# Four sums of weight blocks: from GpSimd additions to accumulating DMAs

## The reference, cut to what matters

```
x = x + mix                     # out_proj "rg_out" (layer 0), "sb_out" (layer 1)
h = rmsnorm(x, norm_ffn_g[layer])
g = h @ w_gate ; u = h @ w_up   # 1024 -> 2816
x = x + (silu(g) * u) @ w_down  # 2816 -> 1024
```

## Time and profile before

| what | value |
|---|---|
| median of three runs | 1937.99 us |
| the profiled execution | 1939.89 us |
| its span | 1938.2 us |
| granted clock, mean | 0.993 |
| TensorE matmuls busy | 1877.3 us, 97% of the span |
| VectorE busy | 1377.6 us, 71% |
| ScalarE busy | 944.6 us, 49% |
| GpSimd busy | 452.3 us, 23% |
| DMA | 174.02 MB, mean 90 GB/s |

### The profile page before, as it was taken

How to read it: one execution, slowest core, us unless ns; L and a number is a source line. 1 busy time by engine, 2 the same in 40 slices (tenths; PEclk the granted TensorE clock), 3 DMA queues, 4 the chain that set the end, 5 groups by cost and what they waited for, 6 DMA issues and landing times.

```text
span 1938.2 us, 30375 instructions
## 1 busy us (share of the span) xinstructions
PE 1877.3 (97%) x10662; PEld 1563.2 (81%) x10662; DVE 1377.6 (71%) x2106; ACT 944.6 (49%) x1573; POOL 452.3 (23%) x426
## 2 busy tenths in 40 slices
PE   9999799999999999979999999999999999999998
PEld 7787689989988777769988998876777887777777
DVE  7687899739965677689964996666667565656553
ACT  6476466415543444546632555345655344444442
POOL 3011555126400000056502530000002045341000
PEclk9999899999999999989999999999999999999999
DMA  7334233233222222223223313211123233232322
GB/s 255 101 96 127 86 98 97 82 114 89 78 96 79 74 61 62 63 87 98 87 98 98 108 57 119 77 55 60 52 86 95 87 89 85 76 87 80 93 82 76
DMA packets 53874, 174.02 MB, mean 90 GB/s; under 512 B 7392, under 2 KB 15712, under 8 KB 53776
## 3 DMA queue, kind: packets, MB, share of 16 engines
q1 hardware_dynamic: 47408, 162.62, 26.8%
q0 software_dynamic: 6368, 10.13, 2.3%
HBM read 168.51 MB, written 4.21 MB: 89 GB/s over the span
## 4 chain that ended last, share of the span: by engine, by line
PE 73%; DVE 11%; issue 4%; ACT 1%; DVEq 0%; ACTq 0%
PE ps L656 15%; PE ps L658 15%; PE ps L657 15%; DVE Wl L2001 4%; PE ps L944 3%; PE tr L910 3%; PE ps L742 3%; PE ps L744 3%; PE ps L743 3%; PE sc L742 2%; PE sc L744 2%; PE sc L743 2%; PE sc L867 2%; DVE Fl L2001 1%; DVE gs L2086 1%
## 5 line engine op out<-in xcount | busy, mean ns | idle before, releaser
L656 PE MATMUL ps<-Hl,Wh 128*128 128x512 f32 x784 | 329.1, 420 | 0.0
L1354 ACT ACTIVATE Wh<-Wr 128x1024 fp32r<-128x1024 f32 (+2 forms) x172 | 195.6, 1139 | 258.7 <-PE ps L658 226.9
L658 PE MATMUL ps<-Hh,Wh 128*128 128x512 f32 x784 | 307.7, 392 | 0.0
L657 PE MATMUL ps<-Hh,Wl 128*128 128x512 f32 x784 | 307.1, 392 | 0.0
L1915 DVE TENSOR_TENSOR Wl<-Wr,Wh 128x1024 fp32r<-128x1024 f32 (+2 forms) x172 | 231.3, 1345 | 102.3 <-ACT Wh L1354 100.8
L656 PE MATMUL ps<-Yl,Wh 128*128 128x512 f32 (+1 forms) x648 | 254.1, 392 | 11.1 <-DVE Wl L1915 7.7
L657 PE MATMUL ps<-Yh,Wl 128*128 128x512 f32 (+1 forms) x648 | 250.8, 387 | 0.0
L658 PE MATMUL ps<-Yh,Wh 128*128 128x512 f32 (+1 forms) x648 | 250.4, 386 | 0.0
L656 PEld LDWEIGHTS ps<-Hl,Wh 128*128 128x128 f32 x784 | 147.8, 188 | 40.3 <-issue 11.1
L742 PE MATMUL ps<-Hl,Wh 128*128 128x256 f32 x528 | 153.8, 291 | 24.9 <-DVE gs L2086 18.8
L2001 DVE TENSOR_TENSOR Wl<-scr,Wh 128x512 fp32r<-128x512 f32 (+1 forms) x132 | 174.5, 1326 | 1.0 <-ACT Wh L1386 1.0
(11 more groups left out here) (405 smaller groups left out, 4326.1 us busy)
## 6 DMA issues: line engine op xcount, KB each, us to landing
Wr<-in_w SPq DMA_DIRECT2D x184, 512.0 KB, 3.6
Wr<-in_w SPq DMA_DIRECT2D x32, 768.0 KB, 4.1
scr<-in_w SPq DMA_DIRECT2D x44, 512.0 KB, 3.6
Wr<-in_w SPq DMA_DIRECT2D x16, 640.0 KB, 3.8
scr<-in_rpb POOLq DMA_DIRECT2D x128, 24.0 KB, 2.1
X<-in_x SPq DMA_DIRECT2D x8, 256.0 KB, 4.2
Wr<-in_wri SPq DMA_DIRECT2D x4, 512.0 KB, 3.5
out_t<-X SPq DMA_DIRECT2D x8, 256.0 KB, 2.5
```

The costliest lines, as they stand in the source:

```text
L656: pe.matmul(bank[:, 0:n], hi, rl[:, k, :], start=(k == 0), stop=False)
L657: pe.matmul(bank[:, 0:n], lo, rh[:, k, :], start=False, stop=False)
L658: return pe.matmul(bank[:, 0:n], hi, rh[:, k, :], start=False, stop=(k == kc - 1))
L1354: act.activation(place(Wh, slot, kc), place(Wr, slot, kc), ACT.Copy).then_inc(w_hi, 1)
```

## The change

GpSimd's `tensor_tensor` additions of weight blocks go. For each sum, SP loads one block (256 KB) into the sum's buffer, and GpSimd then issues a DMA that adds another block to it (`accum_op=ALU.add`): S3 and S1 take the second block from HBM, S2 adds S1's buffer to it, S4 adds S2's buffer, both from SBUF. Such a DMA only adds, so the signs change: the buffers now hold S3 = gate1 + up1, S2 = gate1 + S1, S4 = gate2 + S2. The host does not change any sign; the activations' quarters get other signs (`odd_quarters` uses a column of minus the norm's gain, made once by VectorE), and the down projection's result is subtracted from `X`.

The halves of a weight row are now its first and last 512 columns (before: even and odd chunks), so that each block is one run per partition. For that the chunks of `X` finish in the order 0, 4, 1, 5, 2, 6, 3, 7 (`CHUNK`). `sum3` has two buffers now, `sum2` one as before. GpSimd no longer adds the squares; VectorE does, after each chunk. The queue of SP has 6 loads per pair (512 KB once, 256 KB five times) for 2 of 512 KB.

```diff
+MINUS = {"ffn0": "memg", "ffn1": "mix0"}
+CHUNK = [0, 4, 1, 5, 2, 6, 3, 7]
...
-        raw_w = [(part(7168, KD, P), part(8192, KD, P)),
-                 tuple(Wr[:, q, 0:KD * P].rearrange("p (k c) -> p k c", k=KD) for q in range(2))]
-        raw_rows = raw_w
-        raw_w = [[r.rearrange("p (j e) c -> p e j c", e=2) for r in two] for two in raw_w]
-        sum3, sum2 = scr[:, 9216:9728], scr[:, 9728:10240]
+        raw_a = [scr[:, 7168:8192], Wr[:, 0, 0:2 * S]]
+        raw_22 = [scr[:, 8192:8704], Wr[:, 1, 0:S]]
+        sum3, sum2 = [scr[:, 8704:9216], scr[:, 9216:9728]], scr[:, 9728:10240]
...
+        def summed(p0, h, par):
+
+            return 8 * (h - par) + (8 * p0 + 16)
...
+                p0, landed, rows = PAIR0[name], 8 * b - SKIP[name], a[f"w{KD}"]
+                corner = (b - 5, b - 5) if name.endswith("a") else (b - 1, b)
+
+                def scr_free():
+                    if name.endswith("a"):
+                        sp.wait_ge(x_ok, X0[PAIR_OUT[name]] + 1)
+                    else:
+                        sp.wait_ge(w_lo, b - 7)
+
+                def blocks(h, par):
+                    gate, up = rows[2 * h + row], rows[2 * h + (row + 1)]
+                    lo_at = split_at(h - 2, pairs) if h > 1 else {}
+                    if h < 2:
+                        scr_free()
+                    else:
+                        sp.wait_ge(w_lo, b + lo_at["S3"])
+                    sp.dma_start(sum3[par], gate[:, 0:S]).then_inc(s3_in[par], 16)
+                    if h == 1:
+                        sp.wait_ge(w_lo, b - 1)
+                    elif h > 1:
+                        sp.wait_ge(w_lo, b + lo_at["A"])
+                    sp.wait_ge(w_in[0], 16 * h + landed)
+                    sp.dma_start(raw_a[par], gate).then_inc(w_in[0], 16)
+                    if h == 1:
+                        sp.wait_ge(w_lo, b)
+                    elif h > 1:
+                        sp.wait_ge(w_lo, b + lo_at["A22"])
+                    sp.wait_ge(w_in[1], 16 * h + landed)
+                    sp.dma_start(raw_22[par], up[:, S:2 * S]).then_inc(w_in[1], 16)
+
...
+                blocks(0, 0)
                 for h in range(pairs):
-                    load_pair(h, h % 2)
+                    par = h % 2
+                    if h < 2:
+                        sp.wait_ge(w_lo, corner[h])
+                    else:
+                        sp.wait_ge(w_lo, b + split_at(h - 2, pairs)["S1"])
+                        sp.wait_ge(s2_ok, 16 * (p0 + h - 1))
+                    sp.dma_start(sum1[par], rows[2 * h + (row + 1)][:, 0:S]).then_inc(s1_in[par], 16)
+                    if h + 1 < pairs:
+                        blocks(h + 1, 1 - par)
+                    gate = rows[2 * h + row]
+                    if h > 0:
+                        sp.wait_ge(w_lo, b + split_at(h - 1, pairs)["S2"])
+                        sp.wait_ge(s4_ok[1 - par], summed(p0, h - 1, 1 - par))
+                    sp.dma_start(sum2, gate[:, 0:S]).then_inc(s2_in, 16)
+                    if h > 1:
+                        sp.wait_ge(w_lo, b + split_at(h - 2, pairs)["S4"])
+                    sp.dma_start(sum4[par], gate[:, S:2 * S]).then_inc(s4_in[par], 16)
...
-                    load(u0 + 1, 1, w[row + 1])
+                    load(u0 + 1, 1, w[row + CHUNK[1]])
                     sp.wait_ge(w_hi, u0 + 1)
-                    sp.dma_start(place(Wr, CORNER, KD), w[row + 2].rearrange("p (s c) -> p s c", s=2)).then_inc(w_in[0], 16)
-                    load(u0 + 3, 1, w[row + 3])
-                    it0 = 2
+                    sp.dma_start(place(Wr, CORNER, KD), w[row + CHUNK[2]].rearrange("p (s c) -> p s c", s=2)).then_inc(w_in[0], 16)
+                    for m in range(3, KD):
+                        load(u0 + m, m % 2, w[row + CHUNK[m]])
+                    continue
...
+            def weight_sums(name):
+
+                p0, row, pairs = PAIR0[name], first_row[name], FFA if name.endswith("a") else FFB
+
+                def third(h, par):
+                    pool.wait_ge(s3_in[par], summed(p0, h, par))
+                    pool.dma_start(sum3[par], a[f"w{KD}"][2 * h + (row + 1)][:, 0:S], accum_op=ALU.add).then_inc(s3_ok[par], 16)
+
+                third(0, 0)
+                for h in range(pairs):
+                    par = h % 2
+                    pool.wait_ge(s1_in[par], summed(p0, h, par))
+                    pool.dma_start(sum1[par], a[f"w{KD}"][2 * h + (row + 1)][:, S:2 * S], accum_op=ALU.add).then_inc(s1_ok[par], 16)
+                    if h + 1 < pairs:
+                        third(h + 1, 1 - par)
+                    pool.wait_ge(s2_in, 16 * (p0 + h + 1))
+                    pool.wait_ge(s1_ok[par], summed(p0, h, par))
+                    pool.dma_start(sum2, sum1[par], accum_op=ALU.add).then_inc(s2_ok, 16)
+                    pool.wait_ge(s4_in[par], summed(p0, h, par))
+                    pool.wait_ge(s2_ok, 16 * (p0 + h + 1))
+                    pool.dma_start(sum4[par], sum2, accum_op=ALU.add).then_inc(s4_ok[par], 16)
+
+            for name in ("gu0a", "gu0b", "gu1a", "gu1b"):
+                weight_sums(name)
...
+                elif tag == "S2":
+                    act.wait_ge(s2_ok, 16 * h + (16 * p0 + 16))
                 else:
-                    act.wait_ge(sum_ok, 4 * h + (4 * p0 + {"S3": 1, "S1": 2, "S2": 3, "S4": 4}[tag]))
+                    act.wait_ge({"S1": s1_ok, "S3": s3_ok, "S4": s4_ok}[tag][par], summed(p0, h, par))
...
-                dve.tensor_tensor(tE[e][:, 256:512], tE[e][:, 512:768], tE[e][:, 0:256], ALU.subtract).then_inc(t1_ok, 1)
+                dve.tensor_tensor(tE[e][:, 256:512], tE[e][:, 0:256], tE[e][:, 512:768], ALU.subtract).then_inc(t1_ok, 1)
...
-                n, e, gain = 4 * (nrm == "ffn1") + m // 2, m // 2 % 2, v_col(nrm, m)
+                n, e, c = 4 * (nrm == "ffn1") + m // 2, m // 2 % 2, CHUNK[m]
+                minus = v_col(MINUS[nrm], c)
                 if nrm == "ffn0" and m == 1:
                     dve.wait_ge(mv_st, 64)
+                    dve.wait_ge(neg_ok, 2)
                 dve.wait_ge(x_ok, X0[AFTER[nrm]] + m + 1)
                 dve.wait_ge(t1_ok, n + 1)
-                dve.scalar_tensor_tensor(tO[e][:, 0:512].rearrange("p (a b) -> p a b", a=2),
-                                         X[:, m, 256:512].unsqueeze(1).to_broadcast([P, 2, 256]), gain,
-                                         tE[e][:, 256:768].rearrange("p (a b) -> p a b", a=2), ALU.mult, ALU.subtract)\
+                dve.scalar_tensor_tensor(tO[e][:, 0:256], X[:, c, 256:512], minus, tE[e][:, 256:512], ALU.mult, ALU.subtract)\
                     .then_inc(tt_ok, 1)
+                dve.scalar_tensor_tensor(tO[e][:, 256:512], X[:, c, 256:512], v_col(nrm, c), tE[e][:, 512:768],
+                                         ALU.mult, ALU.subtract)
                 dve.wait_ge(tt_ok, n + 1)
-                dve.scalar_tensor_tensor(tO[e][:, 512:768], X[:, m, 0:256], gain, tO[e][:, 0:256], ALU.mult, ALU.subtract)\
+                dve.scalar_tensor_tensor(tO[e][:, 512:768], X[:, c, 0:256], minus, tO[e][:, 0:256], ALU.mult, ALU.subtract)\
                     .then_inc(te_ok, 1)
...
-                        dve.tensor_tensor(X[:, m, :], X[:, m, :], xr[:, :], ALU.add).then_inc(x_ok, 1)
+                        dve.tensor_tensor(X[:, m, :], X[:, m, :], xr[:, :], ALU.subtract).then_inc(x_ok, 1)
...
-                        dve.tensor_tensor(X[:, m, :], X[:, m, :], ps[bank][:, :], ALU.add).then_inc(x_ok, 1)
+                        c = CHUNK[m] if name in ("rg_out", "sb_out") else m
+                        dve.tensor_tensor(X[:, c, :], X[:, c, :], ps[bank][:, :], ALU.add).then_inc(x_ok, 1)
...
+                    if pairs_in and nrm:
+                        add_square(nrm, m)
...
+            for norm, home in MINUS.items():
+                dve.tensor_scalar(vec[:, VEC[home]:VEC[home] + KD], vec[:, VEC[norm]:VEC[norm] + KD], -1.0, None, ALU.mult)\
+                    .then_inc(neg_ok, 1)
```

More of the change, by code:

```diff
@@ L280, in program @@
         ps += [ctx.enter_context(nc.psum_tensor(f"ps{i}", [P, S], F32)) for i in range(6, 8)]
+        first_row, _rows = {}, {}
+        for _name, _k, _n in STREAM:
+            first_row[_name] = _rows.get(_k, 0)
+            _rows[_k] = first_row[_name] + _n
         def place(w, slot, kc):
@@ L367, in weight_source @@
         def weight_source(tag, par):
-            if tag == "A":
-                return raw_w[par][0]
-            if tag == "A22":
-                return raw_w[par][1][:, 1]
-            return block4({"S1": sum1[par], "S2": sum2, "S3": sum3, "S4": sum4[par]}[tag])
-        def weight_view(w, tag):
-            return weights(w, tag).rearrange("p (e j c) -> p e j c", e=2, j=4) if tag == "A" else block4(weights(w, tag))
+            return {"A": raw_a[par], "A22": raw_22[par], "S1": sum1[par], "S2": sum2, "S3": sum3[par], "S4": sum4[par]}[tag]
+        def summed(p0, h, par):
+            return 8 * (h - par) + (8 * p0 + 16)
```

(55 more changed lines are left out.)

41 lines of the change are left out of this document (13 added, 28 removed).

## The result

The changed kernel takes 2092.26 us (median of 4 runs, 2090.03 to 2094.25) against 1937.88 us (4 runs, 1937.24 to 1940.19) for the kernel before on the same chip. The ratio is 1.0794 with a 95% interval of 1.0775 to 1.0813: 154 us slower. The forecast was 1902 us with a range up to 1985, so it was wrong in sign and outside the range.

What follows compares the result with a forecast made beforehand. The prediction took VectorE, delayed by GpSimd's additions, to bound the loop over pairs: 1939.9 us less 28 (loops) and 8 (heads) is 1904 profiled, 1902 for the median; own range 1894 to 1912, 8 in 10 from 1894 to 1985.

Steps and rivals of the forecast that it cites:

- What bounds the kernel now: Loop over pairs in the `gu` stages: VectorE takes 11.06 us a pair, TensorE needs 10.0, so VectorE bounds by 1.06.
- What the change removes: `gu` loops: without GpSimd's additions VectorE's list falls to about 7.0 us a pair; gain counted as 28 us.
- The head of an FFN: Start of each FFN: gain of 4 us per layer, 8 in all, after charging VectorE's eight additions of squares.
- What it adds, a ring of DMAs: `sum2` in the loop: load, add of S1, add to `sum4`, then next load; 10.2 us, within 10.6 before TensorE waits.
- R: Length of the `sum2` ring, L + 2D + three starts: 10.2 us, with ends 8.2 and 12.2.
- L: SP's 256 KB load from HBM into `sum2`: about 3.1 us.
- D: Accumulating DMA of 256 KB from SBUF to SBUF: 3.3 us, including 0.5 for sharing the queues.
- three starts: Starts after released waits in the `sum2` ring: about 0.16 us each, 0.5 in all.
- The price of R: Loops: beyond about 11.4 us, each us of R costs some 36 us.
- Rival 1: `sum2` ring too slow, D of 4.3 and more: 1959 us, or 2009 at D = 5.0; chance 0.26.
- Rival 2: The 16 DMA engines become the bound, 12.8 us a pair if additions count twice: 1980 us; chance 0.12.
- "DVE blocks DMA" trap: GpSimd's DMA issues: could be longer while VectorE runs 2-port operations; rows show no such delay, no price given.

Runs made afterwards that it cites:

- experiment 1: Kernel before, with GpSimd's four sums of a pair made in 4 of their 512 columns, the rest left out: 1889.45 us, ratio 0.9748.
- experiment 2: Kernel before, with the sums of all pairs but each stage's first two moved from GpSimd to VectorE: 1913.56 us, ratio 0.987.
- experiment 3: Kernel before, with GpSimd's sums of only each stage's first two pairs made over 4 of 512 columns: 1925.06 us, ratio 0.9936.
- experiment 8: Changed kernel, with S2 and S4 of all pairs but a stage's first made by VectorE, their loads and adds gone: 1893.42 us.
- bare ring: Changed kernel, with A and A22 loaded, and S1 and S3 loaded and added, in 16 columns only from the third pair on: 1900.65 us.
- Experiment 5: Changed kernel, with a second `sum2` buffer and the next S1 and S3 adds issued before GpSimd waits for S2: 2001.58 us, ratio 1.0331.
- experiment 6: Three runs of the changed kernel with 16 columns only of A and A22 (2017.83 us), of S1 and S3 (1957.0 us), or of both (1900.65 us).
- experiment 7: Changed kernel, with GpSimd's four DMAs writing over their target instead of adding: 1958.12 us, ratio 1.0105.

## Why the prediction was wrong, by its own steps

**What bounds the kernel: right.** VectorE was the bound, GpSimd's additions stretched it (experiments 1 to 3), and TensorE's own pace was 10.07 us a pair (experiments 1 and 8) where 10.0 was read.

**What the change removes: right, sized low.** The subtractions with 512 columns are at 0.69 us in the mean of the stretch. VectorE's list has 7.4 us a pair (14.86 us busy in two pairs) where 7.0 was forecast. The loops could give 35 us: experiment 1 took 11.1 and 6.6 us from the two of a layer. 28 were counted. Some of the difference is a miscount: 75 products were put between the first and the last read of `gu0a`, 107.3 us, and experiment 1 took 104.5, because its first two reads stand 5.3 us apart. The 87.2 us for `gu0b` came out at 87.7.

**The head of an FFN: right in kind, half the size.** 4 us a layer were counted, and 8.5 us is what the first read came earlier. El fell from 1681 to 956 ns and Hl from 1525 to 745, as estimated. The mistake was to charge VectorE's eight additions of squares against it. They are hidden: the first read comes at 236.3 in the changed kernel, which has them on VectorE, and in experiment 3, which has them on GpSimd. Both undersized terms speak for the change, so they did not make the miss.

**What it adds, a ring of DMAs: this is the step that failed.** R = L + 2D + three starts was the right sum, and the bare ring's links add up to 10.1 us where 10.2 was predicted. That this is so close is in part luck: the load took 2.5 us and not 3.1, the starts 0.8 and not 0.5. And it is a ring alone. L was taken as 3.1, from loads with little beside them, and is 5.1 us in the changed kernel. D was 3.3 for both adds. S4's add does take 3.4, but S2's takes 5.7 in the median and up to 7.4 in the rows above. The starts are not 0.16 each: GpSimd's after a landing is 0.28 and 0.51. R came to 5.1 + 0.3 + 6.7 + 0.5 + 3.4 = 16.0, with 6.7 for the mean of 7.41 and 5.91. The allowance for sharing was 0.5 us on D and none on L, though the same text listed 1 MB of loads shortly before and, under its second rival, that the added work might take 12.8 us of the engines' time in every pair. Those two findings stood side by side and were not put together. With 12.8 us of work for the engines in a period of 10, by its own count, no transfer could be expected to take the time it has alone. The upper end of R, 12.2, was formed with transfers alone as well, and so the range missed.

The price of R was near: 4.9 us over the 11.06 of before at 36 us each is 178, and the loops lost 169.

**Rival 1** (ring too slow) was the right mechanism, at R = 13.6 for its worst case. **Rival 2** (engines the bound) had the right engine time, 12.8 against 12.6. It gave 1980 because it let the ring turn at that pace. Experiment 5, which loosens the ring and the list, comes to 13.6 us a pair and 2002 us, held by the second circle, which no rival named. Both act at once: the adds load the engines, which goes with longer transfers, and a circle adds the lengthened ones up. Experiment 8 shows that a share of 0.75 without the ring of `sum2` is harmless, and experiment 6 that the ring alone is, too.

The Trainium skill's rule, told there of ReduceScatter, that an addition needs two source reads and so runs at half the rate (Collectives: The Full Stack, why ReduceScatter is half of AllGather) agrees with experiment 7: the queue's share goes from 8.9% of 1961.6 us to 15.9% of 2092.6, 1.9 times the engine time for the same bytes. 10 MB of them add in neither run; without these (2.3% of 1938.2 us in the kernel before) it is 2.2 times. That the second read is the reason is not shown: the trace also counts 31712 packets with the addition and 20448 without. The prediction used the rule by name for the duration of one transfer only. The load on the engines it counted twice in rival 2, but not in R.

The "DVE blocks DMA" trap (the Trainium skill, SBUF — State Buffer) was given no price, and none was found: GpSimd's issue did get longer, but the run without additions has plain issues of 0.54 us beside the same VectorE work, so it goes with the addition.

**Open.** A third buffer for `sum1`, which would open the second circle, was not tried. So it is not shown how far the 13.6 us of experiment 5 would fall before the engines' time holds the loop; their share was 0.83 there. Nor was another placing of the loads tried, with A and A22 issued away from S2's add.
